# Gating, squaring and normalising the output projection's first token tile inside the attention stage

## What is computed

```python
# attention: per head, for each block of 128 queries
p = softmax(q @ k.T * scale)                  # two maps
o = (p[0] - lam * p[1]) @ v                   # (128, 4 heads, 128)
att = rms_norm(o, attn_subln_g) * (1 - lam0)  # per head
# scan output y (128, 512), gate z (128, 512)
ssm = rms_norm(y * silu(z), ssm_norm_g)
x = x + gate1 * (concat([att, ssm]) @ w_out)
```

## Time and profile before

| | |
|---|---|
| median of 3 runs | 1336.99 us (1331.07 to 1341.86) |
| the profiled execution, device time | 1345.51 us |
| its span in the trace | 1343.8 us |
| granted TensorE clock, mean | 0.918 of full |

### The profile page before, as it was taken

One profiled execution on the slowest core, in us unless ns is written; L12 is line 12 of the kernel. 1 busy time (PEld: TensorE's weight loads), 2 busy tenths in 40 slices (PEclk: granted clock), 3 DMA queues, 4 the chain that ended last, 5 costly groups with the idle time before them and its releaser, 6 DMA issues. The chain is left out here.

```text
span 1343.8 us, 19190 instructions
## 1 busy us (share of the span) xinstructions
PE 1115.2 (83%) x5908; PEld 932.5 (69%) x5908; DVE 847.3 (63%) x1243; ACT 653.7 (49%) x1081; POOL 473.7 (35%) x275
## 2 busy tenths in 40 slices
PE   4799999979885796988996799947988999899900
PEld 1687777759885695888886688836767877678700
DVE  0763544015554485776765566657898879899668
ACT  2651112114222473666665466414777778768522
POOL 0000000030001293467773000003677678768650
PEclk9899999989998897999999799966999999999955
DMA  9428587131000904354201523134967896733374
GB/s 354 137 98 289 170 277 247 56 106 40 17 0 3 229 21 123 55 130 110 67 32 45 178 96 125 63 111 157 344 234 252 296 348 225 253 135 114 126 267 171
DMA packets 127091, 204.90 MB, mean 152 GB/s; under 512 B 19264, under 2 KB 89824, under 8 KB 124974
## 3 DMA queue, kind: packets, MB, share of 16 engines
q1 hardware_dynamic: 118108, 176.90, 40.1%
q0 software_dynamic: 7344, 26.74, 5.7%
q10 hardware_dynamic: 1570, 0.38, 0.2%
HBM read 215.61 MB, written 45.01 MB: 194 GB/s over the span
## 5 line engine op out<-in xcount | busy, mean ns | idle before, releaser
L88 DVE TENSOR_TENSOR moe_wgu_lo<-moe_wgu,moe_wgu_hi 128x1024 fp32r<-128x1024 f32 x132 | 225.5, 1745 | 39.2 <-ACT moe_wgu_hi L2150 20.9
L88 POOL TENSOR_TENSOR moe_wd_lo<-moe_wd,moe_wd_hi 128x1024 fp32r<-128x1024 f32 x66 | 190.1, 2902 | 70.7 <-ACT moe_wd_hi L2156 70.5
L2150 ACT CAST moe_wgu_hi<-moe_wgu 128x1024 fp32r x132 | 131.7, 1051 | 52.5 <-DMA moe_wgu<-in_w_exp_up 52.2
L93 PE MATMUL moe_gu_ps<-moe_wgu_hi,moe_xT_hi 128*128 128x512 f32 x264 | 111.4, 422 | 17.1 <-DVE moe_xT_lo L88 17.0
L93 PE MATMUL proj_acc_ps<-proj_w_hi,hidden_hT_hi 128*128 128x512 f32 x288 | 118.2, 410 | 6.7 <-DVE hidden_hT_lo L88 6.7
L95 PE MATMUL proj_acc_ps<-proj_w_hi,hidden_hT_lo 128*128 128x512 f32 x288 | 114.8, 399 | 0.0
L94 PE MATMUL proj_acc_ps<-proj_w_lo,hidden_hT_hi 128*128 128x512 f32 x288 | 114.5, 398 | 0.0
L1278 POOL TENSOR_TENSOR att_e<-att_e 128x1152 f32<-128x1152 f32 (+1 forms) x36 | 86.1, 2390 | 72.2 <-DVE att_e L1345 72.2
L95 PE MATMUL moe_gu_ps<-moe_wgu_hi,moe_xT_lo 128*128 128x512 f32 x264 | 107.5, 407 | 0.0
L94 PE MATMUL moe_gu_ps<-moe_wgu_lo,moe_xT_hi 128*128 128x512 f32 x264 | 107.5, 407 | 0.0
L1296 ACT ACTIVATE att_e<-att_sc_ps,att_shift 128x1152 f32<-128x1152 f32 (+1 forms) x72 | 81.4, 1131 | 39.2 <-DVE att_shift L1334 39.0
(11 more groups left out here) (356 smaller groups left out, 2730.6 us busy)
## 6 DMA issues: line engine op xcount, KB each, us to landing
moe_wgu<-in_w_exp_gate SPq DMA_DIRECT2D x34, 1024.0 KB
moe_wgu<-in_w_exp_up SPq DMA_DIRECT2D x34, 1024.0 KB
moe_wd<-in_w_exp_down SPq DMA_DIRECT2D x34, 1024.0 KB
scratch_y_slots<-moe_y SPq DMA_DIRECT2D x33, 512.0 KB
proj_raw<-in_w_in SPq DMA_DIRECT2D x32, 256.0 KB, 5.2
proj_feat<-in_w_ada SPq DMA_DIRECT2D x4, 2048.0 KB, 8.9
proj_xh<-in_w_ada SPq DMA_DIRECT2D x4, 2048.0 KB, 8.9
scratch_h<-late_h SPq DMA_DIRECT2D x9, 512.0 KB, 2.9
```

What stands on the lines that cost most here:

```text
L88: return eng.tensor_tensor(low, value, high.bitcast(F32), ALU.subtract)
L93: pe.matmul(out, a_high, b_high, start=start, stop=False)
L2150: act.copy(wgu_hi[:, k.buf, j:j + 2], wgu[:, buf, j:j + 2]).then_inc(gu_hi_done, 1)
```

## The change

The tiles z and y now belong to the surrounding scope (`W["mix_z"]`, `W["mix_y"]`), so that the attention can use them too. Inside the attention:

- SP loads z and y of tiles 0 and 1 behind the last slices of `w_out` (`load_zy`).
- ScalarE squares heads 0 and 1 of tile 0 at the start of its step 34, heads 2 and 3 at the start of step 35 (`head_square`; the values themselves go to `w_out_raw`, which no one uses by then). In step 36, after it has copied item 34, it takes the Silu of z (`gate_rows`), waits for VectorE's product and squares that (`ssm_square`). After step 37 (item 35 copied) it takes the square root.
- VectorE multiplies y by the gate at the start of its step 37, ahead of `finish` of item 34. Behind the last `finish` (item 35) it waits for the root and runs `normalise` for tile 0.

In the mixer, these instructions of tile 0 and the first four DMAs are gone. TensorE's list begins, as before, with `turn_mix(0)`, and `gate_rows(1)` now stands behind `mix_high(0)`.

```diff
@@ attention_stage, sync: behind load_w_out(sp, I, W, range(4, KT))
+            load_zy(sp, W, M, 0)
+            load_zy(sp, W, M, 1)
@@ attention_stage, scalar
             for k in range(N + 2):
+                if N - 2 <= k < N:
+                    act.wait_ge(o_out, (HEADS - 1) * TILES + 1)
+                    act.wait_ge(W["w_out_split"], KT + 1)
+                    for h in range(2 * (k - N + 2), 2 * (k - N + 3)):
+                        head_square(act, junk[:, h * P:(h + 1) * P], o_tok[:, 0, h * P:(h + 1) * P], first_ms[:, h:h + 1])
                 if k >= 2:
                     evacuate(items[k - 2], 0)
...
                 if k < N:
                     exponential(items[k], 1)
+                if k == N:
+                    gate_rows(act, W, 0)
+                    act.wait_ge(W["gated"], 1)
+                    ssm_square(act, W["mix_z"][:, 0], W["mix_y"][:, 0], first_ms[:, HEADS:])
+            act.drain()
+            act.activation(first_r[:], first_ms[:], ACT.Sqrt, bias=epsc[:, 0:1]).then_inc(first_sq, 1)
@@ attention_stage, vector
             for k in range(N + 3):
+                if k == N + 1:
+                    gated_rows(dve, W, 0)
                 if k >= 3:
                     finish(items[k - 3])
...
+            dve.wait_ge(first_sq, 1)
+            normalise(dve, W, 0, first_r[:], first_ms[:], first_tmp[:])
@@ mixer_stage, sync
-            load_zy(0)
-            load_zy(1)
             for cond in range(2):
                 load_mods(gate, cond, GATE1, gate_in)
@@ mixer_stage, scalar
-            gate_rows(0)
-            mean_squares(0)
-            gate_rows(1)
             mix_high(0)
+            gate_rows(act, W, 1)
             mean_squares(1)
@@ mixer_stage, vector
             router_weights()
-            gated_rows(0)
-            normalise(0)
-            gated_rows(1)
             mix_low(0)
-            normalise(1)
+            gated_rows(dve, W, 1)
+            rooted(1)
```

`rooted(t)` is the wait for the root and then `normalise`. The new functions are those that the mixer had inside it:

```diff
+def load_zy(sp, W, M, t):
+    sp.dma_start(W["mix_z"][:, t % 2], M["z"][t * P:(t + 1) * P, :]).then_inc(W["z_in"][t % 2], 16)
+    sp.dma_start(W["mix_y"][:, t % 2], W["y"][t * P:(t + 1) * P, :]).then_inc(W["y_in"][t % 2], 16)
+def gate_rows(act, W, t):
+    act.wait_ge(W["z_in"][t % 2], 16 * (t // 2 + 1))
+    act.activation(W["mix_z"][:, t % 2], W["mix_z"][:, t % 2], ACT.Silu).then_inc(W["silu_done"], 1)
+def gated_rows(dve, W, t):
+    y = W["mix_y"][:, t % 2]
+    dve.wait_ge(W["silu_done"], t + 1)
+    dve.wait_ge(W["y_in"][t % 2], 16 * (t // 2 + 1))
+    dve.tensor_tensor(y, W["mix_z"][:, t % 2], y, ALU.mult).then_inc(W["gated"], 1)
+def head_square(act, junk, o, mean):
+    act.activation(junk, o, ACT.Square, scale=P ** -0.5, accum_out=mean)
+def ssm_square(act, junk, y, mean):
+    act.activation(junk, y, ACT.Square, scale=DSSM ** -0.5, accum_out=mean)
+def normalise(dve, W, t, r, ms, tmp):
+    y = W["mix_y"][:, t % 2]
+    dve.reciprocal(r, r)
+    refine(dve, r, ms, 1.0, tmp)
+    heads = W["o_tok"][:, t].rearrange("p (h d) -> p h d", h=HEADS)
+    dve.tensor_tensor(heads, heads, bcast(r[:, 0:HEADS], P, 2), ALU.mult)
+    dve.tensor_scalar(y, y, r[:, HEADS:], None, ALU.mult).then_inc(W["mix_done"], 1)
```

More of the change, by code:

```diff
@@ L1231, in attention_stage @@
         inv, ratio = s.sb("inv", [P, 4, 2]), s.sb("ratio", [P, 4])
+        first_ms, first_r, first_tmp = (s.sb(k, [P, HEADS + 1]) for k in ("first_ms", "first_r", "first_tmp"))
+        junk, epsc = W["w_out_raw"], s.sb("epsc", [P, 1])
+        eps_done, first_sq = s.sem("eps_done"), s.sem("first_sq")
         sc = [s.ps(f"sc{m}", 3 * 512) for m in range(2)]
@@ L1316, in _ @@
                     exponential(items[k], 1)
+                if k == N:
[4 more added lines that the diff above has]
+            act.activation(first_r[:], first_ms[:], ACT.Sqrt, bias=epsc[:, 0:1]).then_inc(first_sq, 1)
         @block.vector
         def _(dve):
+            dve.memset(epsc[:], EPS).then_inc(eps_done, 1)
             dve.wait_ge(lam_in, 64)
@@ L1500, in mixer_stage @@
         router_in, gate_in, mods_in = s.sem("router_in"), s.sem("gate_in"), s.sem("mods_in")
-        z_in, y_in, x_in = ([s.sem(f"{k}{u}") for u in range(2)] for k in ("z_in", "y_in", "x_in"))
-        eps_done, silu_done, gated, sq_done, mix_done = (s.sem(k) for k in ("eps_done", "silu_done", "gated", "sq_done", "mix_done"))
+        x_in = [s.sem(f"x_in{u}") for u in range(2)]
+        eps_done, sq_done, gated, mix_done = s.sem("eps_done"), s.sem("sq_done"), W["gated"], W["mix_done"]
         t1_done, mixT_high, mixT_done = s.sem("t1_done"), s.sem("mixT_high"), s.sem("mixT_done")
@@ L1516, in _ @@
         def _(sp):
[L1517 to L1522, removed]
             def load_x(t):
@@ L1563, in _ @@
             act.wait_ge(eps_done, 1)
-            def gate_rows(t):
-                act.wait_ge(z_in[t % 2], 16 * (t // 2 + 1))
-                act.activation(z[:, t % 2], z[:, t % 2], ACT.Silu).then_inc(silu_done, 1)
             def mean_squares(t):
                 for h in range(HEADS):
-                    act.activation(junk[:, h * P:(h + 1) * P], o_tok[:, t, h * P:(h + 1) * P], ACT.Square, scale=P ** -0.5,
-                                   accum_out=ms[:, t % 2, h:h + 1])
+                    head_square(act, junk[:, h * P:(h + 1) * P], o_tok[:, t, h * P:(h + 1) * P], ms[:, t % 2, h:h + 1])
                 act.wait_ge(gated, t + 1)
-                act.activation(junk[:, DATT:], y[:, t % 2], ACT.Square, scale=DSSM ** -0.5, accum_out=ms[:, t % 2, HEADS:HEADS + 1])
+                ssm_square(act, junk[:, DATT:], y[:, t % 2], ms[:, t % 2, HEADS:])
                 act.drain()
@@ L1608, in _ @@
                 if t + 2 < TILES:
-                    gate_rows(t + 2)
+                    gate_rows(act, W, t + 2)
                     mean_squares(t + 2)
@@ L1699, in _ @@
                 if t + 2 < TILES:
-                    gated_rows(t + 2)
-                    normalise(t + 2)
+                    gated_rows(dve, W, t + 2)
+                    rooted(t + 2)
             gate_half(TILES - 1, 1)
@@ L2357, in build @@
                 W["gcol"], W["gains_in"] = m.sb("gcol", [P, KT]), m.sem("gains_in")
+                for k in ("z_in", "y_in"):
+                    W[k] = [m.sem(f"{k}{u}") for u in range(2)]
+                for k in ("silu_done", "gated", "mix_done"):
+                    W[k] = m.sem(k)
                 W["mod_cols"], W["cols_in"] = m.sb("mod_cols", [P, 5, KT]), m.sem("cols_in")
```

23 lines of the change are left out of this document (9 added, 14 removed).

## The result

The changed kernel takes 1330.46 us in the median of 20 runs (1323.81 to 1340.36), the kernel before 1337.24 us (20 runs, 1329.81 to 1342.36). The ratio is 0.9948, 95% interval 0.9929 to 0.9968, so by the ratio the change is worth 7.0 us, between 4.3 and 9.5 (the medians lie 6.8 us apart). The forecast was 1329.2 us and a gain of 7.8.

What follows compares the result with a forecast made beforehand. The prediction took TensorE's 12.17 us idle hole between attention and mixer as the bound: 8.2 - 0.2 (attention's tail) - 0.2 (third tile) = 7.8 us gained, median from 1336.99 to 1329.2 us, range 1321 to 1336.5.

Steps and rivals of the forecast that it cites:

- The hole and its chain: From the attention's last `finish` to tile 0's transposes in the mixer: 3.6 us in place of 11.78, a gain of 8.2.
- Squares of the heads: In ScalarE's attention steps: a pair with readout takes some 0.7 us, hidden in 0.92 us of idleness, 0.2 to spare.
- Silu, product, square of y: In the attention's tail: hidden, 0.5 us spare behind the product and 0.35 behind the square; loss 0.2, bounds 0 to 1.0.
- Loads and memset at nothing: Four 256 KB loads behind the last `w_out` slice and a small memset at the start: nothing waits behind them, no cost.
- Second tile: In the mixer: tile 1 ready at 746.1, wanted by TensorE at 747.2; hidden, 1.1 us to spare.
- Third tile: In the mixer: ScalarE waits up to 6 us for z of tile 2; residual fits by 0.2; loss 0.2, bounds 0 to 3.
- rival 1: Thin covers fail, at tile 2's z or in the attention's tail: gain 5.3 us, 1331.7 us; chance 0.20.
- The clock: TensorE at the mixer's start: the clock falls just before tile 0's transposes, so the slow start moves along unchanged.
- Rival 3: At tile 0's transposes the clock is still high or comes back sooner: gain 10.3 us, 1326.7 us; chance 0.10.
- Rival 2: In the attention's tail a table change amid copies takes 2.56 us, not 1.28: gain 6.6 us, 1330.4 us; chance 0.05.
- Rival 4: In the experts a worse clock makes the kernel slower, 1342.7 us at a mean clock of 0.84; chance 0.05.
- Rival 5: Squares bring table loads, or tile 0 waits for something other than z and `normalise`: no gain, 1337 us; chance 0.03.

Runs made afterwards that it cites:

- e1: Kernel before, with only the loads of z and y of tiles 0 and 1 moved into the attention; GpSimd's last addition to tile 0's transposes (junction): 13.73 us.
- e2: Changed kernel with root and `normalise` of tile 0 back in the mixer; GpSimd's last addition to tile 0's transposes (junction): 10.30 us.
- e3: Changed kernel with Silu of tile 0 written to a free PSUM bank of the scores; product 0.69 us, GpSimd's last addition to tile 0's transposes (junction) 8.19 us.
- e4: Changed kernel with the product behind `finish` of item 34 and square of y behind item 35's copies; GpSimd's last addition to tile 0's transposes (junction): 8.26 us.
- e12: e9 plus unread TensorE transposes, 18 behind the last values and 16 between tile 0's transposes and the product; 1328.33 us, ratio to the kernel before 0.9945.
- e7: Changed kernel with 1.5 MB of unread broadcast loads ahead of z and y of tile 2; ScalarE's wait 8.97 us, TensorE idle 2.44 us.
- e9: Changed kernel with z and y of tile 2 issued ahead of the five broadcasts; first transposes to `turn_x2(0)` 30.03 us, 30.07 in the changed kernel.
- e8: e3 plus the root directly behind the square of y and `normalise` ahead of the last `finish`; 1331.45 us, ratio to the kernel before 0.9947.
- e10: The changed kernel unaltered, run again; 1330.59 us in the median of 12 runs, the kernel before 1339.50.

## Why the prediction was right

- **The hole and its chain.** The sum 2.34 + 1.23 + 0.01 = 3.6 us in place of 11.78 held: in the changed kernel the last `finish` ends at 731.51 and the transposes start at 735.04, 3.53 us. TensorE's idle time is 3.92 us, forecast 4.0. e1 and e2 take the 7.9 us apart into 2.7 for the loads, 3.4 for Silu, product and squares, and 1.7 for the root, as expected within 0.1 us.
- **Squares of the heads.** Hidden, as forecast: the copies behind them had 0.34 us left of 0.92.
- **Silu, product, square of y.** This is where I was wrong within the sum. I took 0.69 us for the product from the mixer, where GpSimd does nothing. The changed kernel shows 1.58 us, ending 0.54 us after GpSimd's addition of two SBUF operands. From PSUM it takes 0.69 (e3), and started later it takes 1.01 and ends at the same distance (e4). So it isn't slowed in proportion: by these ends it waits until GpSimd is done. The Trainium skill, page "SBUF — State Buffer", section "SBUF: two separate sides", says that a VectorE instruction with two SBUF inputs and a GpSimd instruction that reads SBUF take a shared pair of ports in turn, for a whole instruction each; the trace agrees, with the 0.54 us left behind GpSimd's end. The spares of 0.5 and 0.35 us were worked out with 0.69 and both failed; with 0.69 (e3) the junction shrinks by 8.24 us, the forecast's 8.2. The loss was 0.4 us, where I took 0.2 with bounds of 0 to 1.0.
- **Loads and memset at nothing.** Nothing waited for them. The attention's stretch up to GpSimd's last addition was 201.4 us before (from the earlier trace rows) and 201.7 after.
- **Second tile.** Hidden, as forecast: `normalise` ended at 745.83, 1.3 us ahead of the transposes, forecast 1.1. e12 shows how near it was: with a product 2 us sooner, tile 1 is late by 0.65 us.
- **Third tile.** The wait was forecast as up to 6 us, 5 to 6 among the signs, and is 4.67. The cover was 1.6 us and not 0.2: I let z land at 756.6 at the latest, and it was there at 755.2. SP issued it 12.3 us after `gate` and not 13.5, but that isn't what set the landing: the DMA engines were full from 747 to 756 (share 1.01, row below), and in e7, where SP issued it 1.5 us later counted from the transposes of tile 0, it landed 4.3 us later, about what 1.5 MB take at the row's 360 GB/s. The likely cause is the megabyte less in the queue, which the prediction named and didn't price; no run takes it alone. The 0.2 us of loss didn't come (e9: nothing to win). That a cover decides there is true (e7), so rival 1 described a mechanism that exists, but it didn't decide. Its other half, spare tenths of the tail that are gone, did happen, for 0.4 us.

```profile
747.00:756.00 9.00, 9.00 (x58) 7.91 (x56) 1.88 (x3) 3.11 (x5) 0.00 (x0) 1.00 1.01 360
```

- **The clock.** The slow start moved along: 1.09 us for the first four transposes, 1.11 before. Rival 3 (clock still high, 2.5 us more) was tested by e12: the clock can be held, but of the 2.1 us at tile 1 only 0.6 reach the routing. Its price was too high, because I took the mixer's later clock as given: the second low stretch doubled.
- **Rival 2**, a table change that costs double: in every trace the root starts 1.29 or 1.30 us after its load does, in the middle of copies too (e8). The drain of the Trainium skill's page "ScalarE: Activation LUTs", section "What ACT_TABLE_LOAD costs", from which the 6.6 us came, is not borne out by any of them.
- **Rival 4**, a worse clock in the experts: 0.87 before and after in the window from routing to the end. **Rival 5**: the change does what it says.
- **The sum.** 8.2 - 0.2 - 0.2 = 7.8; measured in the traces 16.43 - 8.57 - 0.2 = 7.7, with the 0.4 us of the product in it and no loss in the third tile. The runs give 7.0 (4.3 to 9.5), and 1330.46 us lies 1.3 above the forecast. Two mis-sized terms cancel, and that is luck: 0.4 us for the tail instead of 0.2, and nothing for the third tile instead of 0.2. The interval of the runs is too wide to tell 7.7 from 7.0 or 8.2.

## What to carry to other kernels

Measure such a change from a mark ahead of it to a mark behind it in each trace: here the junction repeats to 0.01 us in e7, e9, e10 and e12, while the whole time of the changed kernel varies by 16.5 us over its 20 runs. When an instruction moves beside another engine's work, don't take its duration from a place where that engine idles; look at its operands, and put one in PSUM, or put it behind what is waited for. In e8 1.1 us of delay ahead of the last matmuls cost another 1.2 us by their clock, so check the granted clock before a chain is made longer to shorten what follows.

## What the runs showed of the hardware that I had not expected

- VectorE's product of two SBUF operands ended 0.54 us after GpSimd's addition whether it had started 1.04 or 0.47 us before the addition's end (1.58 and 1.01 us); with one operand in PSUM it took 0.69 us beside it.
- TensorE's clock fell while TensorE was busy: once 0.8 us into the last values, after 1.41 us of idleness ahead of one transpose (e8), and in the mixer with no idle time in any of the windows, for 3.4 us (changed kernel, e9) or 6.8 us (e12). What sets that second fall stays open; e12 only shows that it came earlier and lasted longer when the first was avoided, and e8 that it may not come.
- Routing and experts took 437.8 to 452.8 us with the same instructions and nearly the same mean clock (0.87 to 0.88). The cause of this spread stays open; it is larger than the change.
